# Halves of squares added before the norms' ones products, values ahead of transposes, and eight unread products at the start

## What is computed

```python
def rms_norm(x, g):
    xf = x.astype(jnp.float32)
    y = xf * lax.rsqrt(jnp.mean(xf * xf, axis=-1, keepdims=True) + RMS_EPS)
    return (y * g.astype(jnp.float32)).astype(x.dtype)

def dense_attention(q, k, v, scale):
    ...
        sc = jnp.einsum('bqhd,bkhd->bhqk', qi, k, preferred_element_type=jnp.float32) * scale
        p = jax.nn.softmax(sc, axis=-1)
        return jnp.einsum('bhqk,bkhd->bqhd', p.astype(v.dtype), v)
    ...

def sq_relu_mlp(xn, w1, w2):
    return jnp.square(jax.nn.relu(xn @ w1)) @ w2
```

## Time and profile before

| | |
|---|---|
| median of 3 runs | 1292.99 us (1292.11 to 1293.11) |
| the profiled execution, its own time | 1294.58 us |
| its span, first to last instruction | 1292.8 us |
| TensorE busy | 1253.7 us, 97% |
| VectorE, ScalarE, GpSimd busy | 821.2 us (64%), 622.7 us (48%), 310.6 us (24%) |
| mean granted TensorE clock | 0.989 |
| read from HBM | 205.11 MB, 159 GB/s over the span |

### The profile page before, as it was taken

One profiled execution on the slowest core, in us unless ns is written; L12 is line 12 of the kernel. 1 busy time (PEld: TensorE's weight loads), 2 busy tenths in 40 slices (PEclk: granted clock), 3 DMA queues, 4 the chain that ended last, 5 costly groups with the idle time before them and its releaser, 6 DMA issues.

```text
span 1292.8 us, 23980 instructions
## 1 busy us (share of the span) xinstructions
PE 1253.7 (97%) x10309; PEld 1213.2 (94%) x10309; DVE 821.2 (64%) x1100; ACT 622.7 (48%) x765; POOL 310.6 (24%) x225
## 2 busy tenths in 40 slices
PE   7999998999999999999989999999999999999997
PEld 7877898999999999999889999999999899999997
DVE  6767746655565566666857655487866567555653
ACT  5555455544444445454645534436466446444431
POOL 2300042000012111202350000189211486444000
PEclk9999999999999999999989999999999999999999
DMA  9531345555566655555245556555554355655550
GB/s 265 172 131 66 111 156 158 183 176 196 173 224 204 189 182 158 186 157 183 79 131 185 191 171 193 180 172 162 186 161 134 130 163 164 196 172 188 188 171 33
DMA packets 194711, 214.00 MB, mean 166 GB/s; under 512 B 5235, under 2 KB 182718, under 8 KB 194606
## 3 DMA queue, kind: packets, MB, share of 16 engines
q1 hardware_dynamic: 189518, 204.93, 49.4%
q10 hardware_dynamic: 4896, 7.08, 1.9%
q0 software_dynamic: 192, 0.46, 0.1%
HBM read 205.11 MB, written 1.05 MB: 159 GB/s over the span
## 4 chain that ended last, share of the span: by engine, by line
PE 80%; DVE 7%; ACT 7%; issue 3%; POOL 2%; DMA 1%; ACTq 0%; DVEq 0%; SPq 0%; POOLq 0%
PE ps L507 69%; ACT whi L965 3%; PE ps L638 2%; PE ps L675 2%; PE ps L541 2%; PE ps L646 2%; POOL wlo L2006 1%; DVE wlo L1350 1%; ACT SN L1027 1%; DVE XL L1384 1%; DVE XT L1469 1%; PE ps L525 1%; PE ps L562 1%; DVE BIG L1887 1%; ACT XH L997 0%
## 5 line engine op out<-in xcount | busy, mean ns | idle before, releaser
L1350 DVE TENSOR_TENSOR wlo<-raw,whi 128x2048 fp32r<-128x2048 f32 (+1 forms) x149 | 346.4, 2327 | 219.7 <-ACT whi L965 219.5
L507 PE MATMUL ps<-XH,wlo 128*128 128x256 f32 x1592 | 451.0, 285 | 8.7 <-POOL wlo L2006 8.2
L507 PE MATMUL ps<-XH,whi 128*128 128x256 f32 x1592 | 454.3, 287 | 0.0
L965 ACT ACTIVATE whi<-raw 128x2048 fp32r<-128x2048 f32 (+1 forms) x189 | 359.7, 1904 | 194.2 <-PE ps L507 164.8
L507 PE MATMUL ps<-XL,whi 128*128 128x256 f32 x1592 | 450.3, 284 | 0.0
L507 PEld LDWEIGHTS ps<-XH,wlo 128*128 128x128 f32 x1592 | 306.8, 193 | 10.1 <-POOL wlo L2006 9.2
L507 PEld LDWEIGHTS ps<-XH,whi 128*128 128x128 f32 x1592 | 306.8, 193 | 3.2 <-issue 2.9
L507 PEld LDWEIGHTS ps<-XL,whi 128*128 128x128 f32 x1592 | 306.8, 193 | 0.0
L2006 POOL TENSOR_TENSOR wlo<-raw,whi 128x512 fp32r<-128x512 f32 x160 | 217.3, 1391 | 291.8 <-ACT whi L965 291.7
L507 PE MATMUL ps<-HH,whi 128*128 128x256 f32 x832 | 229.5, 283 | 0.0
L507 PE MATMUL ps<-HL,whi 128*128 128x256 f32 x832 | 229.3, 283 | 0.0
(11 more groups left out here) (229 smaller groups left out, 1581.0 us busy)
## 6 DMA issues: line engine op xcount, KB each, us to landing
raw<-in_mlp_w_dram SPq DMA_DIRECT2D x64, 1024.0 KB, 5.4
raw<-in_od_w_in_dram SPq DMA_DIRECT2D x36, 1024.0 KB, 5.3
raw<-in_w_in_dram SPq DMA_DIRECT2D x24, 1024.0 KB, 5.2
raw<-in_w_ffn_gate_dram SPq DMA_DIRECT2D x12, 1024.0 KB, 5.2
raw<-in_w_ffn_up_dram SPq DMA_DIRECT2D x12, 1024.0 KB, 5.1
raw<-in_w_ffn_down_dram SPq DMA_DIRECT2D x12, 1024.0 KB, 5.1
raw<-in_ev_w_in_dram SPq DMA_DIRECT2D x6, 1024.0 KB, 11.4
TB<-TA ACTq DMA_DIRECT2D x96, 64.0 KB, 4.1
```

Of the source, the lines that this page charges most:

```text
L507: m = pe.matmul(to, l[c][a], r[c][b], start=first and k == 0, stop=last and k == 3 * n - 1)
L965: act.activation(whi_of(n), raw_of(n), ACT.Copy, scale=1.0).then_inc(*tell(s_whi, ("whi", n)))
L1350: dve.tensor_tensor(wlo_of(n), raw_of(n), f32(whi_of(n)), ALU.subtract).then_inc(*tell(s_wlo, ("wlo", n)))
```

## The change

- `sums` (TensorE) multiplies one half instead of two, by default (n=1); only nq, the norm of a latent, keeps two. For n0, mem, n4 and n5 VectorE adds the right half of the accumulator to the left one after its last `add_square`, for n1, n3 and n6 GpSimd does; n7 is as before. The two reordering copies of n2 (L1669) become one addition that reads both halves in the new order.
- In `attend` the values of s-3 stand in front of the transposes of s-2.
- `keep_busy(n)` issues n products of the 128 x 128 ones with themselves into a bank that nobody has taken yet and that nobody reads: five between the first two and the last two pairs of chunks that are turned in, three behind them.

```diff
-            def sums(name, slot, n=2, cols=False, dilated=False):
+            def sums(name, slot, n=1, cols=False, dilated=False):
...
             def attend(first, n, s):
                 if s < n and members(group_of(first + s))[0] == first + s:
                     scores(group_of(first + s))
+                if 0 <= s - 3 < n and members(group_of(first + s - 3))[-1] == first + s - 3:
+                    values(group_of(first + s - 3))
                 if 0 <= s - 2 < n:
                     transposes(first + s - 2)
-                if 0 <= s - 3 < n and members(group_of(first + s - 3))[-1] == first + s - 3:
-                    values(group_of(first + s - 3))
...
+            def keep_busy(n):
+
+                once.wait_ge(*at("ones"))
+                for _ in range(n):
+                    pe.matmul(ps[7][:, 0:P], ones[:, :], ones[:, :], start=True, stop=True)
+
             for c2 in range(4):
+                if c2 == 2:
+                    keep_busy(5)
                 turn_in(("x", c2), [xrow[:, t, :] for t in range(2)], ("x", c2 // 2), c2)
+            keep_busy(3)
...
-                sums("nq", 1)
+                sums("nq", 1, n=2)
...
                 dve.tensor_tensor(acc(slot)[:, 0:w], acc(slot)[:, 0:w], acc(2)[:, 0:w], ALU.add).then_inc(
-                    *tell(s_sum, ("summed", norm, i), *([("norm", norm)] if done else [])))
+                    *tell(s_sum, ("summed", norm, i), *([("norm", norm)] if done and norm == "n7" else [])))
+                if done and norm != "n7":
+                    a = acc(slot)
+                    once.wait_ge(*at(("summed", norm, i)))
+                    dve.tensor_tensor(a[:, 0:S], a[:, 0:S], a[:, S:2 * S], ALU.add).then_inc(*tell(s_sum, ("norm", norm)))
...
-            for c in range(2):
-                m = dve.tensor_copy(acc(2)[:, c * S:c * S + S].rearrange("p (t a n) -> p t a n", t=2, a=8),
-                                    acc(1)[:, c * S:c * S + S].rearrange("p (n a t) -> p t a n", a=8, t=2))
-            m.then_inc(*tell(s_sum, ("norm", "n2")))
+            a, b = (acc(1)[:, c * S:c * S + S].rearrange("p (n a t) -> p t a n", a=8, t=2) for c in range(2))
+            dve.tensor_tensor(acc(2)[:, 0:S].rearrange("p (t a n) -> p t a n", t=2, a=8), a, b, ALU.add).then_inc(
+                *tell(s_sum, ("norm", "n2")))
...
-                pool.tensor_tensor(acc(slot), acc(slot), acc(2), ALU.add).then_inc(
-                    *tell(s_pool_sum, ("summed", norm, i), *([("norm", norm)] if done else [])))
+                a = acc(slot)
+                pool.tensor_tensor(a, a, acc(2), ALU.add).then_inc(*tell(s_pool_sum, ("summed", norm, i)))
+                if done:
+                    once.wait_ge(*at(("summed", norm, i)))
+                    pool.tensor_tensor(a[:, 0:S], a[:, 0:S], a[:, S:2 * S], ALU.add).then_inc(*tell(s_pool_sum, ("norm", norm)))
```

More of the change, by code:

```diff
@@ L745, in rotary_key @@
                     product(b[:, s * S:s * S + S], w, x, ("product", "kr") if s else None)
-                sums("nk", 1, n=1)
+                sums("nk", 1)
             def latent_queries():
```

## The result

The changed kernel takes **1286.24 us** (median of 4 runs, 1282.86 to 1287.44), beside 1293.05 for the kernel before (4 runs, 1292.11 to 1294.77): ratio 0.9935, 95% interval 0.9921 to 0.9949. The prediction was 1290.6 with a range of 1287.5 to 1293.8. The change is faster by two to three times what was forecast, and the time lies outside the range.

The account below looks back on a forecast made before the run. The prediction took TensorE's work as the bound (in flight 97% of the span, 80% of the chain), then its waits and clock. Terms -0.25 - 0.87 + 0.15 - 1.3 + 0.3 - 0.68 + 0.25 = -2.4 us gave 1290.6 us, range 1287.5 to 1293.8.

Parts of the forecast that it names:

- the order is worth nothing: Attention steps where neither values nor transposes wait: putting values ahead of transposes was to change nothing, 0 us.
- step 13: Third layer's attention: values move into the transposes' 2.88 us wait, -0.68 us, leaving a wait near 2.2 us.
- The values that start early: Values starting at the transposes' old place, 615.08 us, wait for their operand's copy: +0.25 us; short waits of 0.2 to 0.4.
- The norms' sum: All norms' halves without keep_busy, old attention order: n0 -0.68, n2 -0.87, n3 +0.15, n4/n5 -1.3, n6 +0.3, so -2.4 us.
- n4 and n5 -1.3: Two neighbouring norms: GpSimd's slab behind them starts 0.87 us earlier, plus 0.4 us more: -1.3 us.
- n1 0: Norm n1: GpSimd's added addition falls mostly into its idle time ahead of its slab, so 0 us.
- n0 -0.25: First norm: mean at about 25.95 instead of 26.18 us, -0.25 us, bounds -0.68 and +1.4.
- n3 +0.15 and n6 +0.3: Norms with GpSimd's addition: n3's slab starts later, +0.15 us; n6 has 0.70 us more before, 0.43 less after, +0.3.
- the delay of 0.5 us: Start, behind keep_busy: VectorE's last copy to XT moves by about 0.5 us, and with it the work up to n0's mean.
- rival 1: Low clock stretches go, around 667 us or behind the wait before 1020.83: one or two, 1288.8 or 1287.0 us; chance 0.27.
- rival 2: Low clock stretches come behind longer waits, likeliest at n6, 1.8 us: one gives 1292.4, two 1294.2 us; chance 0.13.
- Rival 3: GpSimd's half addition at n6 is locked out beside VectorE's work, 2.7 us more: 1293.3 us; chance 0.05.

Follow-up runs that it names:

- halves_vector_only: Changed kernel with n1, n3 and n6 as before, so GpSimd adds no halves and TensorE sums two there: 1284.35 us, ratio 0.9943 to the kernel before.
- values_transp_scores: Kernel before with each attention step in the order values, transposes, scores: 1310.88 us, ratio 1.0146 to the kernel before.

## Why the prediction was wrong

- **"In most steps neither waits, and the order is worth nothing: the same records run."** This is the step that failed. The same records run, but the distance between two of them depends on both. The term was -0.4 us (-0.68 + 0.25) and measured -4.1 (interval 2.6 to 5.7): 0.19 us in each of about twenty steps, 3.8 us, came from the form, and the rest of step 13 came on top and was taken back by new waits. The numbers for it were in the trace: the transposes take 0.58 us from start to start where values follow them, and in the odd layer's next step, between products, 0.35 (479.57 to 479.92 us). The earlier trace rows show the values of the cross attention, which use the whole array, and the earlier trace rows only the start of the transposes, so the places I looked at closest were those without the effect.
- *Step 13:* the values moved into the wait and run at full clock, as predicted, but the transposes' wait behind them is 0.95 us, not 2.2. The softmax itself was ready 1.05 us earlier relative to TensorE: one of VectorE's `BIG<-BIG,TB` ahead of it took 0.69 us where the same one took 1.52 before, beside GpSimd, which is 0.83 of it. *The values that start early* wait 0.27 us at 610.44, as predicted (0.2 to 0.4 us).
- *The norms' sum* of -2.4 us met the measured -2.3 by luck: the clock was lower in those runs, and at an equal clock they bring 4.4 to 5.7 us. The terms weren't right either: n2 -0.87 (arrived, 0.88), n4 and n5 -1.3 (0.44), n1 0 (0.8 less in five traces, 2.3 in one, 4.1 in three), n0 -0.25 (-2.5 over the runs of n0 alone, 0.6 to 4.3 by its interval, at a higher clock), n3 +0.15 and n6 +0.3 (together 1.0007, which their interval doesn't tell from 1). The failed step among them is n1's 0, which let no shift of GpSimd's slab give time back. Mem's wait is 2.85 us and not 2.4, with no cost in its own runs.
- *n4 and n5* failed at "Their start at 857.84 hangs on ScalarE, which waits for the mean chain of both norms; that moves by n4's 0.87 us alone": the chain's first row moved, and one of its VectorE instructions grew by 0.84 us.
- *`keep_busy`* has the mean of n0 at 25.41 and not 25.95: the delay of 0.5 us that was set against it didn't come. In this trace the transposes behind the products ran at the upper level and ended where they did. But in the trace of halves_vector_only they took 1.92 us, ended at 11.10 in place of 10.28, and the mean came at 25.22 all the same, so their end isn't what sets it; the predicted chain from there failed too.
- *The clock:* a low stretch went at 1021 us (rival 1's place), two came, at n6 (rival 2's) and behind mem. The one at step 13 goes with the order (none in nine traces with the short wait, one in each of nine with the long one), so rival 1 was right about this place. By the balance of the changed kernel's runs it gave nothing: mean clock 0.990 over ten runs against 0.991. L562 and L566 have 22 and 20 records, as predicted. *Rival 3* didn't come: n6's half addition took 0.72 us in every trace that has it, while the addition ahead of it took 3.31.
- *The range* was made from waits and clock stretches. No case in it let TensorE's own work change beyond the removed records, so its low end couldn't reach a time that came from there.

## What to carry to other kernels

Before an order of work is called free, read the distance from the start of one kind of matmul to the start of the next for every pair of kinds that the order makes or breaks: here a pair with different forms of the array took 0.20 us, and one with the same form 0.03 from transposes or values to a product and 0.12 from a product to transposes, and moving one block past another took out one such change twenty times. Where VectorE and GpSimd work side by side, a shift of 0.7 us on one of them can cost or give back more than the instruction that made it, so such a term needs a run of its own, and one trace of it is one throw. Before such a run's time is held against a sum, compare the mean granted clocks of the two kernels' runs: here 0.001 of it was 0.8 to 1.3 us, more than several of the terms. Less work ahead of a wait can cost: at n6 the longer wait was followed by a fall of the clock in six traces of ten, the shorter one in none.

## What was not expected of the hardware

- A 128x128 record moved in between 64-column values costs 0.30 us more than the 0.11 it takes behind them; moved in between values that use the whole array it costs nothing more.
- Scores 1.3 us later in a step (values_transp_scores) cost 12 us of idle time on TensorE, although the transposes of the kernel before wait for the softmax only 3 times, 4.5 us.
- The addition of 128x256 on GpSimd takes 0.74 us (0.65 had been taken), and twelve `wlo` pieces behind it 17.7, 19.7 or, without it, 20.8 us, with nothing between.
- The clock column read 1.00 while eight transposes took 1.97 us, and 1.00 while they took 1.04.
